# A mixture-of-experts decoder in float32: the last round of the expert loop written out, and work moved between the engines around it

## The reference

```python
x = layer_norm(DEEPNORM_ALPHA * x + mix, ln1_g[l], ln1_b[l])
ffn = moe_ffn(x, router_w, router_b, moe_w_gate[l], moe_w_up[l], moe_w_down[l])
x = layer_norm(DEEPNORM_ALPHA * x + ffn, ln2_g[l], ln2_b[l])
```

## Time and profile before

| what | us |
|---|---|
| median of three runs | 696.32 |
| profiled execution, its own time | 695.99 |
| its span | 694.2 |
| TensorE busy | 683.0 (98%) |
| VectorE busy | 307.3 (44%) |
| ScalarE busy | 229.5 (33%) |
| GpSimd busy | 56.4 (8%) |
| moved by DMA | 244.04 MB, mean 352 GB/s |

### The profile page before, as it was taken

One profiled execution on the slowest core, in us unless ns is written; L12 is line 12 of the kernel. 1 busy time (PEld: TensorE's weight loads), 2 busy tenths in 40 slices (PEclk: granted clock), 3 DMA queues, 4 the chain that ended last, 5 costly groups with the idle time before them and its releaser, 6 DMA issues.

```text
span 694.2 us, 13450 instructions
## 1 busy us (share of the span) xinstructions
PE 683.0 (98%) x5516; PEld 408.4 (59%) x5517; DVE 307.3 (44%) x561; ACT 229.5 (33%) x432; POOL 56.4 (8%) x58
## 2 busy tenths in 40 slices
PE   9999999999999999999999999999999999999994
PEld 8989988864335335335379987887433533533531
DVE  5689956687111112112067677778711111111214
ACT  4566567152111112112173656716211111211211
POOL 2025100010000000000025000001000000000001
PEclk9999999999999999999999999999999999999998
DMA  8999334989999999999999743498999999999991
GB/s 311 311 373 397 139 121 182 406 336 423 398 422 422 419 422 419 409 422 419 415 386 390 272 157 124 180 389 343 414 414 422 421 411 422 419 406 421 421 414 68
DMA packets 51030, 244.04 MB, mean 352 GB/s; under 512 B 6233, under 2 KB 6450, under 8 KB 26418
## 3 DMA queue, kind: packets, MB, share of 16 engines
q1 hardware_dynamic: 50994, 243.55, 87.7%
HBM read 242.49 MB, written 1.05 MB: 351 GB/s over the span
## 4 chain that ended last, share of the span: by engine, by line
PE 91%; DVE 7%; issue 1%; ACT 1%; DVEq 0%; ACTq 0%
PE ps L2200 32%; PE ps L1960 11%; PE ps L1955 9%; PE ps L2214 8%; PE ps L2231 8%; PE ps L2181 5%; PE ps L2162 4%; DVE ring_lo L1214 2%; PE ps L1922 2%; PE ps L2170 1%; PE ps L1873 1%; PE ps L2128 1%; PE ps L2268 1%; PE ps L1895 1%; PE ps L1980 1%
## 5 line engine op out<-in xcount | busy, mean ns | idle before, releaser
L2200 PE MATMUL ps<-weights,scratch 128*32 128x512 f32 (+1 forms) x1536 | 167.8, 592 | 0.1
L2200 PEld LDWEIGHTS ps<-weights,scratch 128*32 128x32 f32 x1536 | 49.9, 110 | 114.0 <-issue 114.0
L1214 DVE TENSOR_TENSOR ring_lo<-weights,w_hi 128x2048 fp32r<-128x2048 f32 x35 | 83.1, 2392 | 9.2 <-ACT w_hi L818 9.0
L1730 DVE TENSOR_TENSOR scratch<-ps,early 128x512 f32<-128x512 f32 x16 | 11.0, 690 | 168.1 <-PE ps L2200 168.1
L818 ACT ACTIVATE w_hi<-weights 128x2048 fp32r<-128x2048 f32 x34 | 64.8, 1913 | 23.4 <-PE ps L1960 11.5
L1711 DVE SCALAR_TENSOR_TENSOR rounded<-ps,gslot,rounded 128x512 fp32r<-128x512 f32 x30 | 22.5, 751 | 86.3 <-ACT rounded L1080 86.3
L2200 PE MATMUL ps<-tail,scratch 128*32 128x512 f32 (+1 forms) x512 | 56.4, 592 | 0.0
L1040 ACT ACTIVATE scratch<-ps,ln_col 128x256 f32<-128x256 f32 (+1 forms) x40 | 19.4, 541 | 86.9 <-PE ps L2181 84.6
L1080 ACT ACTIVATE rounded<-ps,gslot 128x512 fp32r<-128x512 f32 x30 | 20.6, 688 | 82.9 <-PE ps L2231 41.5
L1058 ACT ACTIVATE early<-ps 128x512 f32<-128x512 f32 x16 | 9.6, 598 | 98.8 <-PE ps L2200 98.8
L2200 PEld LDWEIGHTS ps<-tail,scratch 128*32 128x32 f32 x512 | 16.6, 110 | 38.3 <-issue 38.3
(11 more groups left out here) (304 smaller groups left out, 1006.7 us busy)
## 6 DMA issues: line engine op xcount, KB each, us to landing
weights<-in_moe_w_gate SPq DMA_DIRECT2D x64, 1024.0 KB, 13.4
weights<-in_moe_w_up SPq DMA_DIRECT2D x32, 1024.0 KB, 11.7
places<-in_moe_w_down SPq DMA_DIRECT2D x32, 1024.0 KB, 11.8
tail<-in_moe_w_up SPq DMA_DIRECT2D x32, 1024.0 KB, 17.6
weights<-in_moe_w_down SPq DMA_DIRECT2D x32, 1024.0 KB, 11.8
weights<-in_a_w_in SPq DMA_DIRECT2D x15, 1024.0 KB, 12.7
weights<-in_kv_w SPq DMA_DIRECT2D x8, 1024.0 KB, 15.4
weights<-in_a_w_out SPq DMA_DIRECT2D x4, 1024.0 KB, 15.2
```

Of the source, the lines that this page charges most:

```text
L1214: V.tensor_tensor(low_part(i), ring[:, piece_slot(i), :, :], w_hi[:, i % HI, :, :].bitcast(F32), ALU.subtract).then_inc(lo_ready, 1)
L2200: last = mm(ps[rows, bank, :], own[:, HALF_K * part + k, rows], w, start=part == 0 and k == 0, stop=part == 1 and k == HALF_K - 1)
```

## The change

1. TensorE's fourth round of the expert loop is written out behind a loop of three. In it `gather` has 128 moving columns instead of 256, and ScalarE and VectorE take half as wide a tile (`gathered_columns`); the down products of the last pair go part by part instead of by banks; the branch around the adding up falls away.
2. `pick_first` is two instructions, one for each token tile, and `gather_first` waits for each tile, and for each half of `xn`, by itself. The zeros multiplied before it have fewer columns.
3. ScalarE normalises all four quarters of `xn`; GpSimd none.
4. VectorE counts the rounds directly after the gates, then takes the gathered half, then makes `xr_lo`.
5. Piece 20: its low part is made by VectorE, between the first and the second half of x; ScalarE rounds piece 20 after the last pair and piece 21 after x; TensorE takes the products in the usual order.
6. Before `turn_normed` there are 14 zero products of 128 columns and 73 of 64 instead of 40 and 29.

```diff
...
+        def gathered_columns(two):
+            return slice(0, 2 * SLOTS if isinstance(two, int) and two == PAIRS // 2 - 1 else 4 * SLOTS)
...
-                pool.wait_ge(ln_stat, 2 * layer + 1)
-                pool.tensor_scalar(xn[:, 1, COLS:D].rearrange("p (k n) -> p k n", k=HALF_K),
-                                   x[:, 1, COLS:D].rearrange("p (n k) -> p k n", k=HALF_K), mv[:, 1, 0:1], rs[:, 2, 1:2],
-                                   ALU.subtract, ALU.mult).then_inc(x_done[1], 1)
...
-                    i = A_PIECES
-                    pool.wait_ge(hi_ready, i + 1)
-                    pool.tensor_tensor(low_part(i), ring[:, piece_slot(i), :, :], w_hi[:, i % HI, :, :].bitcast(F32),
-                                       ALU.subtract).then_inc(lo_ready, 1)
...
-                        if last_pair and part == layer == 0:
-                            high(A_PIECES)
...
-                    high(A_PIECES + 1)
+                    high(A_PIECES)
...
+            normalise_for_experts(0, 1, 1)
...
+            high(A_PIECES + 1)
...
-                V.tensor_tensor(pick[:, :, 4:8, :].rearrange("p t (e h) s -> p t e (h s)", e=2),
-                                iota[:, 0:SLOTS].unsqueeze(1).unsqueeze(1).to_broadcast([P, TT, 2, SLOTS]),
-                                of_pair(slot, 0).unsqueeze(3).to_broadcast([P, TT, 2, SLOTS]),
-                                ALU.is_equal).then_inc(pick_ready, 1)
+                for t in range(TT):
+                    V.tensor_tensor(pick[:, t, 4:8, :].rearrange("p (e h) s -> p e (h s)", e=2),
+                                    iota[:, 0:SLOTS].unsqueeze(1).to_broadcast([P, 2, SLOTS]),
+                                    of_pair(slot, 0)[:, t, :].unsqueeze(2).to_broadcast([P, 2, SLOTS]),
+                                    ALU.is_equal).then_inc(pick_ready, 1)
...
+                count_rounds(layer)
+                take_xe(gathered(layer, 0, 0), range(4, 8), columns_of(0))
                 dve.wait_ge(xr_ready, 2 * layer + 1)
                 V.tensor_tensor(xr_lo, xn, xr_hi.bitcast(F32), ALU.subtract).then_inc(xr_ready, 1)
-                take_xe(gathered(layer, 0, 0), range(4, 8), columns_of(0))
-                count_rounds(layer)
...
-                if half == 1:
-                    dve.wait_ge(lo_ready, A_PIECES + 1)
-                    low(A_PIECES + 1)
+                low(A_PIECES + half)
...
-                for number in (0, 2, 1) if i == A_PIECES else range(3):
-                    w, xs = products[number]
+                for number, (w, xs) in enumerate(products):
...
-                    nothing(BANK_C, COLS // 2 if n < (4, 0)[layer] else COLS // 4)
+                    if n < 6:
+                        nothing(BANK_C, COLS // 2 if n < (2, 0)[layer] else COLS // 4)
+                    else:
+                        mm(ps[:, BANK_C, 0:SHARE], zeros16[:, :], zeros16[:, 0:SHARE], start=True, stop=True)
...
+                    for bank, ready in ((BANK_C, xc_ps), (BANK_D, xe_ps)):
                         for t in range(TT):
-                            last = mm(ps[:, (BANK_C, BANK_D)[k // 4], first:first + P], xn[:, t, k * P:(k + 1) * P],
-                                      pick[:, t, 4:8, :].bitcast(F32).rearrange("p e s -> p (e s)"), start=t == 0, stop=t == TT - 1)
-                        if k == 3:
-                            last.then_inc(xc_ps, 1)
-                    last.then_inc(xe_ps, 1)
-
-                def gather(ks, banks):
+                            if bank == BANK_C:
+                                pe.wait_ge(pick_ready, picked(layer, 0, 0) - 1 + t)
+                            if t:
+                                pe.wait_ge(x_done[1], 2 * layer + 1 + (bank == BANK_D))
+                            for k in range(4):
+                                last = mm(ps[:, bank, k * P:(k + 1) * P], xn[:, t, ((bank == BANK_D) * 4 + k) * P:
+                                                                             ((bank == BANK_D) * 4 + k + 1) * P],
+                                          pick[:, t, 4:8, :].bitcast(F32).rearrange("p e s -> p (e s)"),
+                                          start=t == k == 0, stop=t == TT - 1, skip_group_check=True)
+                        last.then_inc(ready, 1)
...
+                def gather(ks, banks, pairs=2):
+                    width = pairs * 2 * SLOTS
...
+                        first = (j % 2) * width
...
-                            last = mm(ps[:, banks[j // 2], first:first + 4 * SLOTS], part[:, t, k * P:(k + 1) * P],
-                                      pick[:, t, :, :].rearrange("p e s -> p (e s)"), start=n == 0, stop=n == 3)
+                            last = mm(ps[:, banks[j // 2], first:first + width], part[:, t, k * P:(k + 1) * P],
+                                      pick[:, t, 0:4 * pairs, :].rearrange("p e s -> p (e s)"), start=n == 0, stop=n == 3)
...
-                pe.wait_ge(x_done[1], 2 * layer + 2)
-                pe.wait_ge(pick_ready, picked(layer, 0, 0))
...
-                def experts(two, odd):
+                def experts(two, odd, last_pairs=False):
+                    pairs = 1 if last_pairs else 2
...
+                    elif last_pairs:
+                        add_up(0)
+                        add_up(1)
...
-                    if odd:
+                    if odd and last_pairs:
+                        pe.wait_ge(ht_ready, pair + 1)
+                        out_of_hidden(two, odd, 0, who)
+                        out_of_hidden(two, odd, 1, who)
+                    elif odd:
...
-                with pe.Fori(0, PAIRS // 2, 1) as two:
+                with pe.Fori(0, PAIRS // 2 - 1, 1) as two:
                     experts(two, 0)
                     experts(two, 1)
+                experts(PAIRS // 2 - 1, 0, last_pairs=True)
+                experts(PAIRS // 2 - 1, 1, last_pairs=True)
...
-            for _ in range(40):
+            for _ in range(14):
                 nothing(BANK_A, COLS // 4)
-            for _ in range(29):
+            for _ in range(73):
                 mm(ps[:, BANK_A, 0:SLOTS], zeros16[:, :], zeros16[:, 0:SLOTS], start=True, stop=True)
...
```

More of the change, by code:

```diff
@@ L500, in picked @@
         def picked(layer, two, odd):
-            return (PAIRS // 2 + 1) * layer + two + (2 if odd else 1)
+            return (PAIRS // 2 + 2) * layer + two + (3 if odd else 2)
         def turn_place(k):
@@ L1061, in experts @@
                     if not odd:
-                        take_xe(xe_ps, gathered(layer, two, 0) + 1, BANK_C, (0, 1), slice(0, 4 * SLOTS))
+                        take_xe(xe_ps, gathered(layer, two, 0) + 1, BANK_C, (0, 1), gathered_columns(two))
                     act.wait_ge(ht_ps, pair + 1)
@@ L1066, in experts @@
                     if not odd:
-                        take_xe(xe_ps, gathered(layer, two, 0) + 2, BANK_B, (4, 5), slice(0, 4 * SLOTS))
+                        take_xe(xe_ps, gathered(layer, two, 0) + 2, BANK_B, (4, 5), gathered_columns(two))
                     act.wait_ge(put_ps, pair + 2)
@@ L1192, in _ @@
             normalise_for_experts(2, 1, 0)
+            normalise_for_experts(2, 1, 1)
             moe(1)
@@ L1732, in experts @@
                     if not odd:
-                        take_xe(gathered(layer, two, 0) + 1, (2, 3), slice(0, 4 * SLOTS))
+                        take_xe(gathered(layer, two, 0) + 1, (2, 3), gathered_columns(two))
                     if not odd:
-                        take_xe(gathered(layer, two, 0) + 2, (6, 7), slice(0, 4 * SLOTS))
+                        take_xe(gathered(layer, two, 0) + 2, (6, 7), gathered_columns(two))
                     dve.wait_ge(gslot_ready, pair + 1)
@@ L2166, in gather_first @@
                 def gather_first():
-                    for k in range(KT):
-                        first = (k % 4) * P
+                    for bank, ready in ((BANK_C, xc_ps), (BANK_D, xe_ps)):
                         for t in range(TT):
-                            last = mm(ps[:, (BANK_C, BANK_D)[k // 4], first:first + P], xn[:, t, k * P:(k + 1) * P],
-                                      pick[:, t, 4:8, :].bitcast(F32).rearrange("p e s -> p (e s)"), start=t == 0, stop=t == TT - 1)
-                        if k == 3:
-                            last.then_inc(xc_ps, 1)
-                    last.then_inc(xe_ps, 1)
-                def gather(ks, banks):
+                            if bank == BANK_C:
[10 more added lines that the diff above has]
+                    width = pairs * 2 * SLOTS
                     for j, k in enumerate(ks):
-                        first = (j % 2) * 4 * SLOTS
+                        first = (j % 2) * width
                         terms = [(t, part) for t in range(TT) for part in (xr_hi, xr_lo)]
                         for n, (t, part) in enumerate(terms):
-                            last = mm(ps[:, banks[j // 2], first:first + 4 * SLOTS], part[:, t, k * P:(k + 1) * P],
```

(9 more changed lines are left out.)

## The result

The changed kernel takes 699.48 us (median of 7 runs, 698.35 to 699.83) against 696.05 us for the kernel before in the same rounds: 1.0046 of it, interval 1.0036 to 1.0055. Predicted were 696.4 us, a range of 692.9 to 698.2, and "no change" as the likeliest; the measured time lies above the range. The profiled execution has a span of 697.7 us against 694.2.

The account below looks back on a forecast made before the run. TensorE was taken as the bound, busy 194.00 of 194.00 us in layer 0's expert loop, with loads as full. Terms -0.5 + 0 + 0.1 - 0.2 + 0.7 = +0.1 us gave 696.4 us; range 692.9 to 698.2.

Parts of the forecast that it names:

- Narrow gathers: Expert loop's fourth round: matmuls of 128 moving columns step at the load's pace, 0.112 us for 0.119; -0.5 us in all.
- slow narrow form: Rival, gather matmuls: float32r below 256 columns costs what float32 does, 0.223 us a step; 703.6 us, chance 0.15.
- faster one: Rival, gather matmuls: load no floor, pace follows the columns, 0.056 us a step; 692.9 us, chance 0.14.
- Down products by parts: Last pair's down products: bank C complete 1.72 us later, adding up not delayed, 0.06 us of room; 0.
- Entering the experts: Start of experts: gate load follows ScalarE, which has one more quarter; +0.05 us per layer, +0.1 for both.
- VectorE's new order: Start of experts: count first, copy still in time, a stall in pair 0 goes; -0.11 us per layer, -0.2 for both.
- Between the layers: Piece 20: second and third products wait for low parts, +0.41 and +0.31 us; +0.7 together, once.
- Fewer zero products before `turn_normed` end 0.1 earlier in front of the same wait: 0: Between the layers, before the turned x: fewer zero products end 0.1 us earlier, the same wait follows; worth 0.
- the branch that falls away: Fourth round of the expert loop: dropping the branch around the adding up, with narrower ScalarE and VectorE tiles, worth 0.

Follow-up runs that it names:

- e14: Kernel after with the last pair's down product by banks and 33 zero products of 256 columns before `turn_normed`: 697.40 us, ratio 1.0017.
- e16: Kernel after with 33 zero products of 256 columns before `turn_normed` instead of 14 and 73: 696.15 us, ratio 0.9996.
- e1: Kernel after with the zero products before `turn_normed` as in the kernel before (40 and 29): 699.29 us, ratio 1.0038.
- e2: Kernel before with only the zero products before `turn_normed` changed to those of the kernel after (14 and 73): 696.21 us, ratio 0.9997.
- e9: Kernel after with 35 zero products of 256 columns before `turn_normed` instead of 14 and 73: 696.21 us, ratio 0.9997.
- e10: Kernel after with 35 zero products of 256 columns before `turn_normed` and 24 fewer products at the very start: 696.28 us, ratio 0.9998.
- e6: Kernel after with 31 more zero products at the very start, as many columns: 701.38 us, ratio 1.0070.
- e5: Kernel before with its 34 zero products at the very start written as 10 of 512 columns: 699.73 us, ratio 1.0045.
- e12: Kernel before with its 40 and 29 zero products replaced by 35 of 256 columns: 696.86 us, ratio 1.0005.
- e17: Kernel after with 33 zero products of 256 columns, piece 20 as before but ScalarE's high part ahead of its two copies: 696.30 us, ratio 1.0004.
- e11: Kernel after with 35 zeros of 256 columns, GpSimd's low part of piece 20 back, ScalarE's high part behind its last copy: 698.62 us, ratio 1.0033.
- e7: Kernel after with zero products before `turn_normed` and piece 20 as before, plus 31 more products at the start: 701.31 us, ratio 1.0064.
- e3: Kernel after with piece 20 handled as in the kernel before, zero products still 14 and 73: 700.03 us, ratio 1.0056.
- e8: e7 with ScalarE's high part of piece 20 behind its last copy: 700.74 us, ratio 1.0060.
- e4: Kernel after with both piece 20 and the zero products before `turn_normed` as in the kernel before: 699.06 us, ratio 1.0037.

## Why the prediction was wrong

The forecast named as its own sign of being wrong a time that moves by over 1.4 us at a place not named in it. That is what happened: +3.8 us in a stretch that it put at 0. By its own steps:

- *Narrow gathers*, -0.5: right. 0.111 us for 0.112; no slow narrow form, no faster one. The Trainium skill's figure of about 81 ns ("TensorE: Matmul & The Clock Gate", "Back-to-back issue gap") isn't reached in float32r; the pace is the load's.
- *Down products by parts*, 0: TensorE's side right (copies 0.33 us earlier than forecast). That it buys tolerance was said and given no price; between e14 and e16 it is 1.25 us.
- *Entering the experts*, +0.1: the first gate load stood at 150.41, forecast 150.42, but the stages ahead of it began 0.24 later in this execution (141.54 for 141.30 at ScalarE's first quarter), so the entrance gained 0.2 in layer 0, and layer 1 shows 0.29 up to its first gate product. The forecast was +0.05 a layer, so the term was off by 0.25 and 0.34, to the good.
- *VectorE's new order*, -0.2: right. In pair 0 the turn follows the last gather load by 0.13 us (166.06, 166.19). The two layers' experts are 0.37 and 0.31 us shorter; the gathers and pair 0 were to give 0.36.
- *Between the layers*, +0.7: right, +0.66, with both waits where they were foreseen, 0.32 and 0.24 us for 0.41 and 0.31.
- *"Fewer zero products before `turn_normed` end 0.1 earlier in front of the same wait: 0"*: this is the step that failed. TensorE took 3.22 us more from the adding up to `turn_normed` and 0.57 more from there to piece 20. The wait that ended the stretch wasn't that for x but, for 2.88 us, one for code that wasn't there yet, and the lower clock came behind it. The fewer columns aren't to blame (e1, e2); the working counted products and columns and had no term for the code.
- *The written-out round*: "the branch that falls away" was given 0, and no rival held that straight code has to be read. The page of before showed the queue "instruction" with 24 packets; the question what 8 more would do, and where TensorE runs through its code fastest (zeros of 0.03 us each), wasn't asked.

What is shown: the stop stands at a place in the instructions (53 with either mix of zeros, 22 with 31 products more in front, and 46 in the kernel before with 24 fewer), it ends 2.4 to 2.6 us after an instruction packet starts, and it is gone when TensorE gets to the place later than that (e9, e10, e16), at 696.15 to 696.28 us, within 0.3 of the predicted 696.4. What is open: what starts that packet. It isn't TensorE's coming to the place, since in e6 TensorE stood 1.4 us before it started, and in e10 it started with the place about 6 us ahead. The jump over the overflow rounds fits all nineteen traces. Why a packet starts before that jump in four kernels with the loop kept whole, and not in the fifth (e5), isn't settled; e5 differs from the kernel before only in where its code lies. Whether full load engines delay it (share 1.05) wasn't tried.

## What to carry to other kernels

Count instructions, not only their time: where an engine runs through many short ones (zeros multiplied against idle time), the reading of code can be the bound, and any edit upstream moves the place where it bites. Write such fillers as few, wide products, which bring TensorE later to the place; where the code comes in time it makes no difference (e2, e12). When an unchanged stretch turns slow with idle time that has no releaser, compare the instruction queue's packets of both kernels, and shift the code by a known number of products before blaming the edit.

Before moving work into an engine's idle time, look at what else ends there: a load that lands late (e17), or a port that another engine holds (e11).

## What the runs showed of the hardware

- TensorE's code comes in packets of 16 KB most of which take 0.9 to 1.1 us; after a stop its next instruction follows 2.4 to 2.6 us after the packet's start. Inside the expert loop none comes for 162 us (the kernel before: 190.9 to 352.9).
- In fifteen of nineteen kernels a packet starts 3.4 to 3.6 us after the end of the jump over the overflow rounds, and the jump took 0.35 to 0.37 us; in the four where a packet had started before it, 0.22.
- With a stop of 2.2 to 4.0 us TensorE's clock goes to 0.50 for 3.4 us (6.8 in e7), from inside the stop or up to 1.0 us behind it, in the profiles of after, e1, e3 and e5 to e8, and not in that of e4. What it costs goes by what runs then: `turn_normed` to piece 20 takes 2.27 us in the kernel after and 3.06 in e5, but 1.70 in e8, where the clock had risen before.
- VectorE's TENSOR_SCALAR of 128x2 elements takes 0.17 us alone and 3.66 beside GpSimd's subtraction; BATCH_NORM_AGGREGATE beside it keeps its time.
